# A routed expert block in float32: one more slot for landing weights from step 4 on, two places instead of three for gathered tokens

## The reference, cut to what matters

```python
h = rms_norm(x, norm_mix)
x = x + pool_mixer(h, pool_w, pool_scale)          # trailing windows 2/4/8/16
h = rms_norm(x, norm_ffn)
# router: best group of 4, best two of its 8 experts, softmax gates
...
g_part, up = jnp.split(xblk @ w_gu[e], 2, axis=-1)  # w_gu[e]: 1024 x 1024
yb = (silu(g_part) * up) @ w_dn[e]                  # w_dn[e]:  512 x 1024
out = out.at[buf_tok].add(yb * buf_w)
...
return rms_norm(x, norm_final)
```

## Time and profile before

| what | value |
|---|---|
| median of 3 runs | 662.57 us (661.85 to 663.51) |
| the profiled execution, own time | 663.27 us |
| its span, first to last instruction | 661.5 us |
| PE busy | 622.6 us, 94% |
| DVE busy | 606.2 us, 92% |
| ACT busy | 535.7 us, 81% |
| POOL busy | 157.9 us, 24% |
| memory read over the span | 227.19 MB |

### The profile page before, as it was taken

One profiled execution on the slowest core, in us unless ns is written; L12 is line 12 of the kernel. 1 busy time (PEld: TensorE's weight loads), 2 busy tenths in 40 slices (PEclk: granted clock), 3 DMA queues, 4 the chain that ended last, 5 costly groups with the idle time before them and its releaser, 6 DMA issues.

```text
span 661.5 us, 9555 instructions
## 1 busy us (share of the span) xinstructions
PE 622.6 (94%) x3460; PEld 526.4 (80%) x3460; DVE 606.2 (92%) x501; ACT 535.7 (81%) x458; POOL 157.9 (24%) x127
## 2 busy tenths in 40 slices
PE   6899989999999999999999999897999989989983
PEld 4799978887888888888888888686877868767872
DVE  5887688989999999999999999897989889998987
ACT  5996626688898989898988988887879688978794
POOL 5000010032222222222222222252225222340311
PEclk9999989999999999999999999999999989989997
DMA  8997769999999999999999999999999999999985
GB/s 293 421 418 278 244 209 374 397 343 302 322 381 404 390 400 393 386 401 374 402 367 401 364 401 366 402 379 392 381 384 386 385 413 384 410 409 400 380 335 211
DMA packets 43637, 242.83 MB, mean 367 GB/s; under 512 B 8184, under 2 KB 9344, under 8 KB 19011
## 3 DMA queue, kind: packets, MB, share of 16 engines
q1 hardware_dynamic: 34322, 220.39, 84.2%
q0 software_dynamic: 9264, 21.79, 12.1%
HBM read 227.19 MB, written 26.21 MB: 383 GB/s over the span
## 4 chain that ended last, share of the span: by engine, by line
DMA 54%; PE 34%; DVE 5%; ACT 3%; issue 2%; SPq 0%; POOL 0%; ACTq 0%; POOLq 0%; DVEq 0%
DMA raw<-in_expert_w_gu 32%; PE psum L1724 19%; DMA raw<-in_expert_w_down 17%; PE psum L1736 3%; PE psum L1652 3%; PE psum L1670 2%; DMA total<-ysb,src_all 2%; PE psum L1638 2%; DMA raw<-total 1%; PE psum L1776 1%; DMA pw_in<-in_pool_w 1%; PE psum L1661 1%; DVE raw L1548 1%; PE psum L1678 1%; PE psum L1787 1%
## 5 line engine op out<-in xcount | busy, mean ns | idle before, releaser
L1210 DVE TENSOR_TENSOR w_lo<-raw,w_hi 128x2048 fp32r<-128x2048 f32 x113 | 255.4, 2284 | 7.8 <-ACT w_hi L884 7.4
L884 ACT ACTIVATE w_hi<-raw 128x2048 fp32r<-128x2048 f32 x113 | 213.5, 1914 | 21.8 <-DMA raw<-in_expert_w_gu 12.8
L1210 DVE TENSOR_TENSOR w_lo<-raw,w_lo 128x2048 fp32r<-128x2048 f32 x79 | 178.5, 2283 | 2.4 <-ACT w_lo L884 2.3
L884 ACT ACTIVATE w_lo<-raw 128x2048 fp32r<-128x2048 f32 x79 | 149.5, 1914 | 13.2 <-DMA raw<-in_expert_w_gu 10.2
L710 POOL DMA_INDIRECT total<-ysb,src_all x28 | 53.5, 1910 | 338.5 <-ACT ysb L979 323.9
L1724 PE MATMUL psum<-w_lo,x_hi 128*128 128x512 f32 x432 | 127.1, 397 | 5.8 <-DVE x_lo L1446 5.8
L1724 PE MATMUL psum<-w_lo,h_hi 128*128 128x512 f32 x376 | 108.3, 395 | 0.5 <-DVE h_lo L1480 0.5
L1724 PEld LDWEIGHTS psum<-w_lo,x_hi 128*128 128x128 f32 x432 | 81.0, 190 | 23.2 <-DVE x_lo L1446 6.7
L696 POOL DMA_INDIRECT xg<-normed,src_all x31 | 78.2, 2523 | 21.5 <-DVE src_all L1305 12.3
L1724 PEld LDWEIGHTS psum<-w_lo,h_hi 128*128 128x128 f32 x376 | 70.9, 190 | 15.5 <-DVE h_lo L1480 0.9
L1736 PE MATMUL psum<-w_lo,x_hi 128*128 128x512 f32 x276 | 74.0, 392 | 0.0
(11 more groups left out here) (208 smaller groups left out, 865.4 us busy)
## 6 DMA issues: line engine op xcount, KB each, us to landing
raw<-in_expert_w_gu SPq DMA_DIRECT2D x128, 1024.0 KB, 10.9
raw<-in_expert_w_down SPq DMA_DIRECT2D x64, 1024.0 KB, 11.8
res<-in_x SPq DMA_DIRECT2D x8, 512.0 KB, 9.7
normed<-nx POOLq DMA_DIRECT2D x8, 512.0 KB, 7.3
total<-res SPq DMA_DIRECT2D x8, 512.0 KB, 8.7
raw<-total SPq DMA_DIRECT2D x8, 512.0 KB, 13.4
out<-raw SPq DMA_DIRECT2D x8, 512.0 KB, 3.9
pw_in<-in_pool_w SPq DMA_DIRECT2D x1, 1024.0 KB, 8.1
```

The lines of the kernel that those rows point to most:

```text
L884: nc.scalar.activation(hi_at(s0, j), raw[q][:], ACT.Copy).then_inc(hi_done, 1)
L1210: V.tensor_tensor(w_lo[q][:], raw[q][:], hi_at(s0, j).bitcast(f32), ALU.subtract)\
```

## The change

Places move, one count changes, and a few waits follow from it:

- `XG` is 2 instead of 3. POOL gathers for step s+2 where it gathered for step s+3.
- The third gathered place's room (WORK + 8 KB) becomes `ysb`. The 8 KB at WORK + 28 KB, where ysb and the NFIN tile were, become a fourth high place, `w_more`. So at step 4 only one raw slot is given away (`GIVEN = {HEAD: 1, ...}`): 17 raw slots instead of 16 from pair 35 on, and 15 instead of 14 late. The high places are as many as before.
- `lower` now lies in x_lo's room, and the sum of a small step goes to a tile of its own, `sums`, which lies over silu and hid. `add_lower` waits also for `hid_turned`, and `low_x` behind it waits for `summed`.
- `nfin` and the third late gather go into a raw slot that is free at the end, and wait for `pair_used` to reach 178.

```diff
-    RAW, SPLIT, XG = 18, 3, 3
+    RAW, SPLIT, XG = 18, 3, 2
+    FIRST_GATHERS = 2
...
-    GIVEN = {HEAD: 2, E - 10: 2}
+    GIVEN = {HEAD: 1, E - 10: 2}
...
-        nfin = at("nfin", [P, D], f32, NFIN)
-        lower = at("lower", [P, D], f32, NFIN)
+        w_more = at("w_more", [P, PAIR], f32r, WORK + 28 * KB)
...
+        lower = at("lower", [P, D], f32, WORK + 16 * KB)
+        sums = at("sums", [P, D], f32, WORK + 20 * KB)
...
-        ysb = at("ysb", [P, D], f32, WORK + 28 * KB)
+        ysb = at("ysb", [P, D], f32, WORK + 8 * KB)
...
+            if m == FIRST:
+                in_hi.insert(SPLIT, -1)
...
-            sp.wait_ge(hid_made, LAST_SMALL + 1)
+            sp.wait_ge(pair_used, end_free[TILES // 2 + 1])
             sp.dma_start(nfin[:], norm_final.rearrange("(a d) -> a d", a=1).to_broadcast([P, D]))\
...
             pool.wait_ge(x_turned, E)
+            pool.wait_ge(pair_used, end_free[TILES // 2 + 1])
...
-                nc.scalar.activation(silu[0:H, :], lower[0:H, 0:F], ACT.Silu).then_inc(silu_done, 1)
+                nc.scalar.activation(silu[0:H, :], sums[0:H, 0:F], ACT.Silu).then_inc(silu_done, 1)
...
+                dve.wait_ge(hid_turned, s)
-                V.tensor_tensor(lower[0:H, :], GU[0:H, :], lower[0:H, :], ALU.add).then_inc(summed, 1)
+                V.tensor_tensor(sums[0:H, :], GU[0:H, :], lower[0:H, :], ALU.add).then_inc(summed, 1)
...
+                    if not is_small(s):
+                        dve.wait_ge(summed, small_turn(s - 1, 0) + 1)
                     low_x(s)
```

More of the change, by code:

```diff
@@ L133, in hybrid_pool_moe @@
             in_raw[r], in_hi[h] = m, m
-        end_raw = sorted(range(RAW - SPARE), key=lambda r: in_raw[r])[:TILES // 2 + 1]
+        by_age = sorted(range(RAW - SPARE), key=lambda r: in_raw[r])
+        end_n = next(r for r in by_age if r >= PER_STEP)
+        end_raw = [r for r in by_age if r != end_n][:TILES // 2 + 1] + [end_n]
         end_free = [in_raw[r] + 1 for r in end_raw]
-        END_H = end_raw[TILES // 2]
+        END_H, END_N = end_raw[TILES // 2:]
+        nfin = at("nfin", [P, D], f32, END_N * SLOT)
+        last_late = at("last_late", [P, D], f32, END_N * SLOT + 4 * KB)
         h2_hi = at("h2_hi", [P, KF, P], f32r, END_H * SLOT)
@@ L417, in hi_at @@
             h = hi_of[pair(s0, j)]
-            return w_hi[:, h, :] if h < SPLIT else w_lo[RAW - 1 - (h - SPLIT)][:]
+            return w_hi[:, h, :] if h < SPLIT else w_more[:] if h == SPLIT else w_lo[RAW - 1 - (h - SPLIT - 1)][:]
         def start(s):
@@ L470, in late_tile @@
         def late_tile(k):
-            return xg[:, (E - LATE + k) % XG, :]
+            return xg[:, (E - LATE + k) % XG, :] if k < XG else last_late[:]
         def end_tile(i):
@@ L535, in step @@
                         sp.wait_ge(mixed, TILES)
-                        for g in range(XG - 1):
+                        for g in range(FIRST_GATHERS):
                             sp.wait_ge(gathered[g], 16)
@@ L1457, in low_first_x, with add_lower @@
                         .then_inc(split, 1)
-            def add_lower(turn):
+            def add_lower(s, turn):
                 dve.wait_ge(lower_copied, turn + 1)
-                V.tensor_tensor(lower[0:H, :], GU[0:H, :], lower[0:H, :], ALU.add).then_inc(summed, 1)
+                dve.wait_ge(hid_turned, s)
+                V.tensor_tensor(sums[0:H, :], GU[0:H, :], lower[0:H, :], ALU.add).then_inc(summed, 1)
             def hidden_of_sums(s):
@@ L1467, in hidden_of_sums @@
                 dve.wait_ge(hid_turned, s)
-                V.tensor_tensor(hid[0:H, :], silu[0:H, :], lower[0:H, F:2 * F], ALU.mult).then_inc(hid_made, 1)
+                V.tensor_tensor(hid[0:H, :], silu[0:H, :], sums[0:H, F:2 * F], ALU.mult).then_inc(hid_made, 1)
             def hidden(s, gu=GU):
@@ L1527, in step @@
                 if is_small(s - 1):
-                    add_lower(small_turn(s - 1, 0))
+                    add_lower(s - 1, small_turn(s - 1, 0))
+                    if not is_small(s):
+                        dve.wait_ge(summed, small_turn(s - 1, 0) + 1)
                     low_x(s)
```

## The result

The changed kernel took 675.08 us (median of 4 runs, 672.68 to 677.12), against 662.21 us (661.69 to 663.51) for the kernel before beside it: ratio 1.0175, with a 95% interval of 1.0154 to 1.0197. The sign and the size were forecast (671.6 us, 667.0 to 676.0), with a sum that was too small: +9.0 us said, +11.6 by the ratio (interval 10.2 to 13.0), and 12.9 between the two medians. A later repeat gave 673.08 us against 663.36, ratio 1.0133 [1.0110, 1.0155], so +8.8 us by the ratio and 9.7 between the medians. The profiled execution of the changed kernel has a span of 675.3 us and an own time of 677.12 us; it was the longest of its four runs.

The account below looks back on a forecast made before the run. Bound: when loads begin to run full (about 185 us) plus the bytes after. Stall 9.0 + half clock 1.7 − slot 2.7 + extra gather 1.0 = +9.0 us on 662.57, so 671.6 us, range 667.0 to 676.0.

Parts of the forecast that it names:

- The bound: Loads run full from about 185 us; that time and the bytes after it set the end; later PE has about 18 us slack.
- Part 2, the stall: At 140 us PE waits 9.0 us for step 3's gather, now behind the first scatter; passed on in full.
- Part 2, the half clock: Behind the hole at 140 us PE runs at half clock for 3.4 us, losing 1.7 us.
- Rival A: Step 3's gather lands after 3.8 us, so PE stalls only 2.4 us and the total is 663.3 us; chance 0.05.
- Part 1, the slot: The extra raw slot lets loads issued about 177 to 195 us go one pair earlier: a gain of 2.7 us.
- Part 3, the gathers a step later: The other gathers cause no stall, but one more falls into the full stretch, after 185 us: 1.0 us.
- rival C: A late gather, such as step 22's with 1.5 us margin, lands late, or a first takes 13.5 us: 674.6 us; chance 0.10.
- Part 4: Small sums: DVE's added waits delay PE by up to 2.4 us, inside its slack, so they cost nothing.
- Part 5: The end: the last norm's row waiting for pair 177, the moved `ysb` and the late gather cost nothing.
- The hole, its place, its releaser and the scatter's time: One PE hole of about 9 us at 140 us, ended by step 3's gather; POOL's first scatter still at 136.5 us.
- The hole near 424 us: PE's hole there should be shorter or gone, since PE is later by more than the loads are.
- The sign for a broken margin: If the end moves by more than PE does, a later gather's thin time margin before its turn has broken.

Follow-up runs that it names:

- e5: Kernel before, with 44 rounds of filler matmuls on PE ahead of the turn of step 3's tokens, at 140 us: 672.79 us, ratio 1.0132.
- e6: Kernel before, with the same 44 rounds of filler matmuls ahead of the turn of step 17's tokens, at 368 us: 663.72 us, ratio 1.0002.
- e2: Kernel before, three places and 16 slots, with only the gather of step 3 moved behind the first scatter: 673.75 us, ratio 1.0157.
- e3: Changed kernel with step 3's gather issued before the first scatter, 16 raw slots and no `w_more`: 665.54 us, ratio 1.0032.
- e7: Kernel before, 16 slots and three places, with every gather issued a step later but step 3's early: 665.75 us, ratio 1.0037.
- e8: Changed kernel with POOL's loop reordered, so that each gather goes out ahead of the scatter it stood behind: 661.56 us, ratio 0.9969.
- e11: Changed kernel with POOL's loop reordered, gathers ahead of scatters, and 16 raw slots instead of 17: 664.63 us, ratio 1.0011.
- e9: The changed kernel unaltered, run again beside the kernel before: 673.08 us, ratio 1.0133.
- e4: Changed kernel with 60 rounds of filler matmuls on PE before it waits for the gather of step 3: 677.65 us, ratio 1.0211.
- e10: Changed kernel with 40 rounds of filler matmuls on PE before it waits for the gather of step 3: 674.50 us, ratio 1.0149.

## Why the prediction was right, point by point

**The bound (right).** The end is the time from which the loads run full, plus the bytes after it. e5 and e6 show both halves of it, and the chain after is loads from 240 us on, as the section on the result reads it.

**Part 2, the stall (right).** Forecast 9.0 us, as 138.76 + 10.4 − 140.13. The gather took 10.8 us and PE waited 9.30; in the repeat 9.3 and 7.78, in e2 9.6 and 8.11. The median of the other gathers was the right row, and the longest ones (13.5) were not needed. The latency differs from execution to execution, and the stall with it by the same amount in these profiles. The changed kernel's four runs spread over 4.4 us, but the kernel before spread over 5.6 us in 29 runs beside e5, so the spread by itself shows nothing. Passed on in full: e2 and e5.

**Part 2, the half clock (mechanism right, size too small).** Forecast 1.7 us from 3.4 us at 0.50; it was 2.3 to 2.8. The failed step is taking the length of the low stretch from a hole of 3.49 us: behind this hole 5.7 us were at 0.50, in the repeat 4.9, in e2 5.9. Rival A called 2.4 us too short to lower the clock; in the trace of before no low clock follows the hole of 2.59 us at 423.5, but 3.4 us of it follow one of 2.47 us at 581.9, so that was not safe to say.

**Part 1, the slot (right on the loads' issues).** Forecast 2.7 us; the load issues are 2.7 us earlier in both pairs of kernels. In the run times one pair says about as much (2.8) and the other less (1.2). In the changed kernel itself they are 12.2 − 2.7 = 9.4 us late.

**Part 3, the gathers a step later (the term that was mis-sized).** Forecast 1.0 us, bytes of one gather at 390 GB/s. Measured 2.1 (e3) and 2.5 us (e7) by the ratios, and 3.2 to 4.0 us in the table's column of last landing minus load issues, in the six traces that have the changed kernel's order on POOL from step 4 on (e7, with the same order in the old buffers, has 5.0); that column has single executions, some of them well above the medians of their kernels. The failed step is the claim that the shift costs only the bytes of one gather more in the full stretch. In e8 and e11 each gather from step 5 on stands again where the kernel before had it, no gather more falls into the full stretch, and the same count gives nothing; they have 0.6 us (e8, after the slot's 2.7) and 0.7 by the ratios, 0.8 and 1.0 in the column. So the count fits them within the noise. In the order that was changed it falls short by 1.1 us (e3, at least 0.3) and 1.5 us (e7, at least 0.1). It also misses the manner: one gather more would be lost once and early, while half of e3's loss comes after 390 us. One more thing differs from before in that order: a gather of 128 rows used to follow a scatter of 64 rows and the other way round, and with a step less between them large follows large. e8 and e11 have the old pairing again and no gather more in the full stretch, so they cannot tell the two apart. That the pairing is the cause is argued, not shown; no run here changed it alone. The stalls that a thin margin might have brought (rival C) did not come. The smallest margin in the changed kernel was 1.0 us, at step 24, where the gather held POOL for 6.38 us:

```profile
482.39 6.38 POOL L704 DMA_INDIRECT xg<-normed,src_all  x1 [0.31 <-issue]
...
497.41 1.05 PE L1788 MATMUL psum<-ident,xg 128*128 128x128 f32 x8
```

**Part 4 (right, as far as the intervals go).** e7 has none of the shared tiles and loses as much as e3. **Part 5** shows nothing of its own in any trace.

**The sum.** 9.0 + 1.7 − 2.7 + 1.0 = 9.0 was forecast; the profiled execution reads 9.4 + 2.7 − 2.7 + 3.4 = 12.8, the repeat 7.9 + 2.3 − 2.7 + 3.8 = 11.3. Two small terms were short, both in the same direction, and the range held since it had reached for a longer stall that did not come: that the result lies in it is in part luck. The profiled execution was the longest of its kernel's four; e9's was the longest of its four too.

**What I had said would show it.** The hole, its place, its releaser and the scatter's time are as said. SP's waits for PE between 110 and 200 us grew by 8 us (64.5 to 72.7, both lines of PE together; 7 said). The low clock lasted longer than the 3.4 us said. The hole near 424 us did not go: PE still has one of 2.49 us at 436.5, and 500:600 has 10.1 us of them where before had 6.0. The reason: I had expected PE to be 2.7 us later than the loads, and so to use up the hole; from pair 109 to pair 122, around that hole, it is 12.2 us late and the landings 11.3 to 12.4, the loads having lost by then most of what the slot had given them. The sign for a broken margin, an end that moves by more than PE does, came without one: the last landing is 12.8 us late and PE 12.2, and no gather after that of step 3 came late.

For the one gather that counted, the profiles have 10.8, 9.3 and 9.6 us to landing, with loads in flight. The Trainium skill, page "DMA: Bandwidth & Descriptors", section "Anatomy of one DMA — SWDGE (gpsimd) path", gives about 2.0 us plus the bytes over 436 GB/s, as an estimate 3.2 us for this transfer. These traces do not agree with it there, and the measurement decides.

## What to carry to other kernels

A buffer that is given up shortens a prefetch by one step of *its queue*, and what that costs is decided by what stands ahead of it there: look for an instruction with a long wait (here a scatter that waits 16 us for a result) that the prefetch now comes behind. Then find the time from which transfers run full: a stall before it arrives at the end about one for one, a stall behind it may cost nothing (8.8 us and 0.1 us for the same stall here). In a queue that carries both prefetches and write-backs, try the prefetch ahead of a write-back that waits; here that turned a loss of 1.3 to 1.8% into a gain of 0.3% with the same buffers. Most of it came from one gather: moving that of step 3 alone left a loss of 0.1%.

## What the runs showed of the hardware

- The clock fell to 0.50 (1.2 GHz) inside the hole, 4.7 us after PE's last matmul in the changed kernel and 2.4 us after it in the repeat, and stayed there 10.2 us in either, 5.7 and 4.9 of them behind the hole. PE at work on fillers for 9.1 to 13.6 us in the same place kept 1.00 (e4, e5, e10).
- An indirect gather of 128 rows of 4 KB landed after 9.3 to 11.0 us in all five profiled executions in which it went out behind the first scatter with weight loads in flight, and after 3.6 to 3.9 us in empty queues. The changed kernel's gather of step 5 (64 rows), issued at 169.5 us when the loads had only just started again, took 5.2 us.
- Issuing such a gather mostly holds POOL for 1.8 to 2.5 us, but now and then for 6 us or more: 6.38 us at 482 us, and 8.55 us at the most among the later gathers of the changed kernel. No run here shows why.
